# Queries of a hybrid decoder layer in three rounded passes over weight blocks, two token tiles at a time

## The reference, cut to what matters

```python
q = (xt @ w_query).reshape(t, PEER_HEADS, 2, D_HALF)          # 8 heads x 2 halves x 128
scores = einsum('thpd,hpnd->thpn', q, sub_keys)               # 128 keys in each half
sv, si = top_k(scores, 16)
cand_s = sv[:, :, 0, :, None] + sv[:, :, 1, None, :]          # 256 candidates
top_s, pos = top_k(cand_s, 16);  gate = softmax(top_s)        # 8 x 16 experts a token
a = einsum('ted,td->te', expert_u[idx], x)
out = einsum('te,ted->td', gate * gelu(a), expert_v[idx])     # 16384 experts
```

## Time and profile before

| | us |
|---|---|
| median of 3 runs | 1621.68 |
| lowest and highest | 1615.96, 1624.44 |
| the profiled execution | 1623.71 |
| its span, first to last instruction | 1622.0 |
| TensorE busy | 1559.6 (96%) |
| VectorE busy | 1229.5 (76%) |
| ScalarE busy | 703.1 (43%) |
| GpSimd busy | 397.1 (24%) |
| DMA, moved | 425.78 MB, 263 GB/s over the span |

### The profile page before, as it was taken

One profiled execution on the slowest core, in us unless ns is written; L12 is line 12 of the kernel. 1 busy time (PEld: TensorE's weight loads), 2 busy tenths in 40 slices (PEclk: granted clock), 3 DMA queues, 4 the chain that ended last, 5 costly groups with the idle time before them and its releaser, 6 DMA issues.

```text
span 1622.0 us, 23064 instructions
## 1 busy us (share of the span) xinstructions
PE 1559.6 (96%) x7813; PEld 1329.9 (82%) x7813; DVE 1229.5 (76%) x2273; ACT 703.1 (43%) x1289; POOL 397.1 (24%) x326
## 2 busy tenths in 40 slices
PE   6999889999899999999999999899999999999996
PEld 5777755545599998999999999898888888888885
DVE  5789633398469888898789966458888888888888
ACT  4532533213268634885358833233333333333333
POOL 1004200001023300232003344203334444444430
PEclk9999999999999999999999999999999999999998
DMA  8974700001269975799649999959999999999992
GB/s 315 334 238 138 285 1 0 1 1 53 78 234 357 382 248 170 273 364 349 218 143 344 357 388 363 393 194 343 353 335 358 357 354 343 355 358 356 343 328 94
DMA packets 173078, 425.78 MB, mean 263 GB/s; under 512 B 13373, under 2 KB 62525, under 8 KB 169801
## 3 DMA queue, kind: packets, MB, share of 16 engines
q1 hardware_dynamic: 86704, 265.37, 44.2%
q0 software_dynamic: 36864, 134.23, 23.3%
q10 hardware_dynamic: 49432, 25.19, 5.4%
HBM read 372.32 MB, written 52.43 MB: 262 GB/s over the span
## 4 chain that ended last, share of the span: by engine, by line
PE 86%; DVE 6%; DMA 5%; ACT 1%; issue 1%; ACTq 1%; SPq 0%; DVEq 0%
PE bank L1313 10%; PE bank L1314 10%; PE bank L1317 10%; PE bank L1258 10%; PE bank L1259 10%; PE bank L1260 10%; PE bank L1202 7%; PE bank L1273 5%; PE bank L1185 3%; DMA weights<-in_expert_v 2%; DMA weights<-in_w_ada 1%; PE bank L1212 1%; PE bank L1124 1%; PE bank L1120 1%; PE bank L1032 1%
## 5 line engine op out<-in xcount | busy, mean ns | idle before, releaser
L1258 PE MATMUL bank<-h_hi,u_hi 128*128 128x384 f32 x1024 | 350.3, 342 | 11.9 <-ACT ada L883 6.4
L1259 PE MATMUL bank<-h_lo,u_hi 128*128 128x384 f32 x1024 | 345.0, 337 | 0.0
L1260 PE MATMUL bank<-h_hi,u_lo 128*128 128x384 f32 x1024 | 344.7, 337 | 0.0
L1313 PE MATMUL bank<-v_hi,w_hi 128*128 128x512 f32 x768 | 299.4, 390 | 1.1 <-DVE w_lo L1801 1.1
L1314 PE MATMUL bank<-v_lo,w_hi 128*128 128x512 f32 x768 | 298.8, 389 | 0.0
L976 ACT ACTIVATE v_hi<-weights 128x1024 fp32r<-128x1024 f32 x128 | 135.9, 1061 | 330.9 <-PE bank L1317 291.1
L1699 DVE TENSOR_TENSOR u_lo<-weights,u_hi 128x1024 fp32r<-128x1024 f32 x128 | 156.5, 1222 | 120.9 <-PE bank L1260 87.8
L1317 PE MATMUL bank<-v_hi,w_lo 128*128 128x512 f32 x768 | 236.4, 389 | 0.0
L1797 DVE TENSOR_TENSOR v_lo<-weights,v_hi 128x1024 fp32r<-128x1024 f32 x128 | 157.6, 1231 | 94.8 <-ACT v_hi L976 94.8
L1258 PEld LDWEIGHTS bank<-h_hi,u_hi 128*128 128x128 f32 x1024 | 194.7, 190 | 14.0 <-issue 11.2
L1259 PEld LDWEIGHTS bank<-h_lo,u_hi 128*128 128x128 f32 x1024 | 194.9, 190 | 0.0
(11 more groups left out here) (293 smaller groups left out, 2280.2 us busy)
## 6 DMA issues: line engine op xcount, KB each, us to landing
weights<-in_uT SPq DMA_DIRECT2D x128, 512.0 KB
weights<-in_expert_v SPq DMA_DIRECT2D x128, 512.0 KB, 6.9
gates_dense<-weights SPq DMA_DIRECT2D x24, 1024.0 KB
weights<-gates_dense ACTq DMA_DIRECT2D x16, 1536.0 KB
shared<-gelu_dense SPq DMA_DIRECT2D x64, 384.0 KB, 8.1
shared<-in_w_ada SPq DMA_DIRECT2D x16, 1024.0 KB, 5.4
gelu_dense<-weights SPq DMA_DIRECT2D x32, 384.0 KB
gelu_dense<-ada SPq DMA_DIRECT2D x32, 384.0 KB
```

The lines of the kernel that those rows point to most:

```text
L1258: nc.tensor.matmul(a, uh[:, k, :], h2_hi[:, :, k, :], start=(k == 0), stop=False)
L1259: nc.tensor.matmul(a, uh[:, k, :], h2_lo[:, :, k, :], start=False, stop=False)
L1260: ins = nc.tensor.matmul(a, ul[:, k, :], h2_hi[:, :, k, :], start=False, stop=(k == KC - 1))
L1313: nc.tensor.matmul(acc, wh, v_hi[:, r % 2, cols], start=begin, stop=False)
```

## The change

Queries are made transposed at once, so that no query is turned: the weight block of 128 columns is the stationary operand and two token tiles are streamed, 256 columns. They are made in three rounded passes as the products are. The weights come in 16 blocks of 512 KB from an array laid out by block. A ring of eight blocks (raw and lo in one place, hi in another) is filled at the start of attention. Steps 0 to 15 make tiles 0 and 1, in iterations 35 to 50 of the loop; steps 16 to 31 make tiles 2 and 3 behind it, going back through the blocks, so that eight are still there and eight are loaded a second time. Eight blocks are rounded beside heads 5, 8, ..., 26, eight in iterations 38 to 45, and eight in steps 17 to 24. The normed tokens are split on their way out of their transposes' banks. On VectorE tile 0's selection begins with five segments inside the loop; then come five of tile 1, 15 of tile 0, and the other 15 of tile 1 beside the first 17 products. The selection's scratch, the sub-keys, the one-hot rows, the stored products and the gated values lie elsewhere. The dots, the gate loads of ScalarE and the gating of the sparse weights are spread anew.

```diff
-BESIDE = {1: (0,) * 19 + (3,), 2: (1,) * 18 + (0, 0), 3: (1,) * 18 + (0, 0)}
+BESIDE = {1: (0,) * 5 + (1, 1, 1, 2, 1, 1, 1, 1, 1, 1, 2, 1, 1, 1, 1), 2: (1,) * 10 + (0,) + (1,) * 9, 3: (1,) * 10 + (0,) + (1,) * 9}
+FIRST_REST = 3
-LOOP_AT = 12
+LOOP_AT = 14
-DOTS_AT_SEGMENTS = (2, 5, 8, 11, 14)
-DOTS_PER_BODY = {12: 12, 13: 12, 14: 10}
+DOTS_AT_SEGMENTS = {1: (0,) * 9 + (1, 0) * 5 + (1,),
+                    2: (0, 1, 0, 0) * 5, 3: (0, 1, 0, 0) * 5}
+DOTS_AT_LOOP = (2, 2, 2, 1) * 4
+G_LOADS_AT = {(14, 3): 0, (15, 0): 1}
...
+RING_Q = 8
+PER_GROUP = 4
+PAIR_TILES = ((0, 1), (2, 3))
+STEPS_Q = [(0, p) for p in range(HP)] + [(1, p) for p in reversed(range(HP))]
+FIRST_Q = LAST - HP + 1
+ROUNDED_Q = list(range(HP)) + list(reversed(range(RING_Q)))
+ROUND_Q_AT = {5 + 3 * p: p for p in range(RING_Q)}
+ROUND_Q_AT |= {FIRST_Q + 3 + i: RING_Q + i for i in range(RING_Q)}
+EARLY_SEGMENTS = 5
+EARLY_AT = range(LAST - EARLY_SEGMENTS, LAST)
...
-            for g in (2, 3, 0, 1):
-                load_group("w_query", g)
-            sp.wait_ge(a2_done, 1)
+            for p in range(RING_Q):
+                load_wq(p)
+            wait_full(sp, "O", NT - 1)
             sp.dma_start(keysT, sub_keysT).then_inc(keys_in, 16)
+            for p in range(RING_Q):
+                wait_full(sp, "q", 0, p)
+                load_wq(p + RING_Q)
+            for p in range(HP - 1, RING_Q - 1, -1):
+                wait_full(sp, "q", 1, p)
+                load_wq(p - RING_Q)
...
-            wait_full(sp, "qrow", NT - 1, 0)
+            wait_full(sp, "q", 1, 6)
...
-                                wait_full(pool, "turn", 0)
+                                wait_full(pool, "score", NT - 1, 0)
...
+            def round_wq(s):
+                p, uses = ROUNDED_Q[s], s // RING_Q + 1
+                act.wait_ge(wq_in[p % RING_Q], 16 * uses)
+                nc.scalar.activation(wq_hi[p % RING_Q][:, :, :], wq_raw[p % RING_Q].rearrange("p (k n) -> p k n", k=KC),
+                                     ACT.Copy).then_inc(wq_hi_made, 1)
+            def copy_q(step):
+                b = wait_full(act, "q", *STEPS_Q[step])
+                release(nc.scalar.activation(qT[:, step % 2, 0:2 * P], b[:, 0:2 * P], ACT.Copy), "q", *STEPS_Q[step])
...
+                if n in ROUND_Q_AT:
+                    round_wq(ROUND_Q_AT[n])
+                if n >= FIRST_Q:
+                    copy_q(n - FIRST_Q)
+                if n > FIRST_Q:
+                    copy_scored(n - FIRST_Q - 1)
...
+            for step in range(HP, 2 * HP):
+                if 1 <= step - HP <= RING_Q:
+                    round_wq(HP + step - HP - 1)
+                copy_q(step)
+                copy_scored(step - 1)
+                if step == 2 * HP - 3:
+                    wait_full(act, "q", 1, RING_Q // 2)
+                    for r in range(2):
+                        round_u(0, r, True)
...
+            def queries(step):
+                which, p = STEPS_Q[step]
+                tiles = PAIR_TILES[which]
+                pe.wait_ge(wq_lo_made, p + 1 if which == 0 or p >= RING_Q else HP + RING_Q - p)
...
+                for k in range(KC):
+                    at = slice(k * P, (k + 1) * P)
+                    h_hi = h2_hi_first[:, :, at] if which == 0 else h2_hi[:, 1:3, k, :]
+                    nc.tensor.matmul(both_tiles, w_hi_p[:, k, :], h_hi, start=(k == 0), stop=False)
+                    if which:
+                        nc.tensor.matmul(both_tiles, w_hi_p[:, k, :], h2_lo[:, 1:3, k, :], start=False, stop=False)
+                    else:
+                        for t in tiles:
+                            nc.tensor.matmul(both_tiles[:, t, :], w_hi_p[:, k, :], h2_parts(t)[1][:, k, :], start=False, stop=False)
+                    ins = nc.tensor.matmul(both_tiles, w_lo_p[:, k, :], h_hi, start=False, stop=(k == KC - 1))
+                done(ins, "q", which, p)
+            def score(step):
...
+                for half, t in enumerate(PAIR_TILES[which]):
+                    b = start("score", t, g) if j == first else bank[place["score", t, g][0]]
+                    ins = nc.tensor.matmul(b[:, j * P:(j + 1) * P], qT[:, step % 2, half * P:(half + 1) * P], keysT[:, p, :],
+                                           start=True, stop=True)
...
-                if n in FIRST_QUERY:
-                    query(0, QUERY_PAIRS[FIRST_QUERY[n]])
-                if n == SECOND_QUERY:
-                    for pair in QUERY_PAIRS:
-                        query(1, pair)
-            for n in range(2, NT):
-                for pair in QUERY_PAIRS:
-                    query(n, pair)
+                if n >= FIRST_Q:
+                    queries(n - FIRST_Q)
+                if n > FIRST_Q:
+                    score(n - FIRST_Q - 1)
+            for step in range(HP, 2 * HP):
+                queries(step)
+                score(step - 1)
+            score(2 * HP - 1)
...
+            def rest_of_h2(t):
+                hi, lo = h2_parts(t)
+                for s in range(2):
+                    b = wait_full(dve, "h2T", t, s)
...
+            def rest_of_wq(s):
+                b = ROUNDED_Q[s] % RING_Q
+                dve.wait_ge(wq_hi_made, s + 1)
+                tt(wq_lo[b][:, :, :], wq_raw[b].rearrange("p (k n) -> p k n", k=KC), wq_hi[b][:, :, :].bitcast(F32),
+                   ALU.subtract).then_inc(wq_lo_made, 1)
...
-            for _step in first:
-                pass
+            early = [retrieved[1]] * EARLY_SEGMENTS + [retrieved[0]] * (SEGMENTS - EARLY_SEGMENTS)
+            for i, selection in enumerate(early):
+                next(selection, None)
+                if i % 2 and i // 2 < RING_Q:
+                    rest_of_wq(HP + i // 2)
+                if i == SEGMENTS - FIRST_REST:
+                    rest_of_u(0, 0, True)
...
-                for which, rows in ((1, hot_j), (0, hot_i)):
...
+                keys = turned[:, half * HTOK // P % 2, 0:2, at:at + HTOK]
+                tt(hot[:, half % HALVES], iota128.unsqueeze(1).unsqueeze(1).broadcast_to([P, 2, HTOK, P]),
+                   keys.unsqueeze(3).broadcast_to([P, 2, HTOK, P]), ALU.is_equal).then_inc(hot_made, 1)
...
                 if first:
+                    if m == 0:
+                        sparse_weights()
                     loop_add(J, r)
```

More of the change, by code:

```diff
@@ L536, in load_a @@
                     .then_inc(a_in[b], 16)
-            with sp.Fori(LOOP_AT, FEW_DOTS_AT) as I:
-                for r in range(BODY):
-                    loop_product(I, r, True)
             wait_full(sp, "turn", DENSE - 1)
@@ L1275, in build @@
                     ins.then_inc(built, 1)
-            for g in range(4):
-                wait_read(pe, "score", NT - 1, g)
-            pe.wait_ge(h2_lo_made, DENSE)
             m = 0
@@ L1291, in _ @@
                 if d == 0:
-                    for t in range(NT):
-                        for s in range(2):
-                            wait_read(pe, "h2T", t, s)
+                    for g in range(2):
+                        for t in PAIR_TILES[1]:
+                            wait_read(pe, "score", t, g)
                 for h in range(HALVES * d * CHUNKS, HALVES * (d + 1) * CHUNKS):
```

306 lines of the change are left out of this document (144 added, 162 removed).

## The result

The changed kernel takes 1634.39 us, median of five runs (1633.24 to 1635.49); the kernel before, five runs beside it, 1623.02. The ratio is 1.0072, 95% interval 1.0055 to 1.0089: slower, where 1609 was forecast, and 2 us above the top of the range. The profiled execution took 1634.05 us, its span 1632.3 against 1622.0. The 10.3 us between the spans lie as follows; the forecast column is the prediction's own sum cut at the same points.

What follows compares the result with a forecast made beforehand. The prediction took TensorE, busy 96% of the span, as the bound. Its terms, 9.9 + 7 - 1.5 - 1 - 1.7 = 12.7 us, took the profiled 1623.7 to 1611.0, 1609 in the median's terms; 8-in-10 range 1592 to 1632 us.

Steps and rivals of the forecast that it cites:

- Part 2: Attention: rounding eight weight blocks beside the heads delays its end by 8 us, bounds 2 and 18.
- Rival (d): Attention: every rounding is paid in full, 10 us worse than forecast, 1619 us; chance 0.10.
- Part 1: Query steps on TensorE: 120 us with scores against 136, saving 16 us; steps of 3.6 and 2.9 us without scores.
- Rival (c): Query steps: a 256-column pass costs much more than 120 ns, slower from 146 ns, 1678 us at 213 ns; chance 0.08.
- Rival (e): Queries: three passes for four gain little, 104 against 111 us, had the transposes stayed; no chance given.
- Part 3: Attention's end to first products: product 0 at 428 us, product 1 waiting 3.5 us for VectorE; 9.9 us gained.
- Part 4: Products beside the selections: 7 of 8.7 us of holes and slow clock gained, bounds 3 and 11; selection 1 loses 1.5.
- Part 5: Last two bodies: 11 us of loss against 9.8 before, minus 1; sparse weights behind the first output step, minus 1.7.
- the 9.8 us: Last bodies of the kernel before: a 6.4 us TensorE wait plus 3.4 us lost to half clock.
- 30.9 MB at 400 GB/s: Last 16 products: this traffic, some 28 MB needed in time, takes 70 us against 66, a hole of 4 to 6.
- the like stall: Last bodies: ScalarE's second gate load sticks about as long as the kernel before's 13.35 us; sign given as 10 to 20.
- rival (b): Last bodies: DMA engines bound, ScalarE stands 26 us at body 15; 16 us worse than forecast, 1625 us; chance 0.17.

Runs made afterwards that it cites:

- e1_rest_later: Changed kernel with VectorE's rest of each of attention's eight weight blocks one head after ScalarE's rounding: 1618.37 us, 0.9967 to the kernel before.
- e12_rest_behind: The best version: e10_best with VectorE's rest of each of the sixteen first blocks one iteration after ScalarE's rounding, in the tail: 1595.26 us, 0.9846 to the kernel before.
- e5_ve_order: Changed kernel with attention's roundings moved to the tail, plus VectorE's list at the end of the queries reordered: 1612.73 us, 0.9939 to the kernel before.
- e3_before_19: Kernel before with one product, not three, at selection 1's last segment and 19, not 18, beside selections 2 and 3: 1611.18 us, again 1612.98.
- e10_best: Changed kernel, attention's roundings in the tail, VectorE's lists reordered, nine dots beside selections 2 and 3, sparse weights ahead of the first output step: 1601.12 us, 0.9867.
- e9_thin: Changed kernel with attention's roundings in the tail and first-table gathered rows moving an eighth of their bytes: 1604.62 us, 0.9891 to the kernel before.
- e4_gates_apart: Changed kernel with ScalarE's first gate load issued three products earlier: 1636.11 us, 1.0078 to the kernel before.

## Why the prediction was wrong

The granted clock has two levels here, and half clock is the lower one, 1.2 instead of 2.4 GHz.

**The step that failed is Part 2's sum, "Sum 8 us; bounds 2 (all in present idle time) and 18 (eight times 2.3)".** Attention ended 22.6 us later, 0.7 of it from ahead of attention. That is 14.6 of the 23.0 us by which the total is off, and outside the bounds. The mechanism had been named ("ScalarE's queue holds the next exponentials behind it, VectorE's the next row maximum, and TensorE waits for both"), but each rounding was priced as its 2.3 us of work, less a head of cover. Three things were missing. First, the upper bound counted work and not waits: VectorE waits 19 us for ScalarE beside its own work, because the two stand at the same place in both lists. e1_rest_later changes nothing but that order, and 16 us go. Second, an output projection was taken as cover at head 17, and head 23 was counted at 0.5; but there the rest stands ahead of what the projection and the turn wait for, VectorE's copy (L1610) and head norm (L1585), and TensorE waits 3.09 us at 212.26 and 4.73 at 246.54. Third, the sum had no term for the clock: 4.3 us of the delay are TensorE busy at a lower granted clock (0.92 instead of 0.97). This part the better order did not give back, since e1_rest_later's attention is at 0.92 too; what it gave back is idle time. Rival (d), "attention pays every rounding in full", came nearest, at 18 us still 4 short. With the order of e1_rest_later attention ended 6.3 us later than in the kernel before (275.68 against 269.36), so 8 would have been enough for a good order.

**Part 1, the queries: right.** A step of the first pair takes 3.7 us without its scores, forecast 3.6; one of the second pair takes 3.3 us with them, forecast 3.4. Rival (c), a 256-column pass at 146 ns or more, is out, since 24 passes of 256 columns with their own weights start 0.12 us apart. The rule of the Trainium skill, TensorE: Matmul & The Clock Gate, section The mechanism, that a weight load overlaps a running matmul only on another row group, does not agree with these rows. Rival (e) is answered too: with the transposes gone TensorE is busy 151.6 us in the tail against 165.1.

**Part 3, the tail: right in kind, 5.4 us too good.** Product 0 came 156.0 us after attention's end, forecast 150.6. The sum had TensorE busy throughout; it waits 2.93 us for VectorE's copy and 1.40 for a rest of turned tokens (L1705), and runs at half clock from the end of the first wait, 334.2, to 337.1 (1.5 us lost): 5.8 us. Windows of 10 us with this and with the slow clock after product 1's wait:

```profile
330.00:340.00 10.00, 7.07 (x50) 6.91 (x50) 2.42 (x3) 1.33 (x2) 0.00 (x0) 0.83 0.18 52
450.00:460.00 10.00, 5.99 (x26) 5.67 (x26) 9.86 (x36) 4.41 (x6) 4.43 (x5) 0.83 0.36 118
```

The first of the waits is Part 2's mistake once more: Part 3 priced the rests of the tail by VectorE's room, 25 us against 15, and not by what stands behind each. With them in better places the same tail is 151.5 us (e12_rest_behind, 269.5 to 421.0). Product 1's wait on VectorE was forecast at 3.5 us with half clock behind it; it was 4.0, with half clock from its end, 456.4, to 460.0. VectorE's selection was indeed late next; that it was its order is shown by e5_ve_order.

**Part 4, the selections: too careful.** 8.7 us were counted as 7, of which 1.5 came back in selection 1. e3_before_19 shows 9 to 13 us for the edit alone. In the changed kernel three waits of 1.0 us take some of it back; e10_best shows that two of them came with the dots. What is left is some 7 us against the 5.5 of the sum.

**Part 5, the last two bodies: the total right, the step from before not.** 11 us were forecast. Measured are waits of 1.04, 1.66 and 5.63 us and, from 1058.7 to 1064.2, 5.5 us at half clock, 2.8 lost: 11.1.

```profile
1057.00:1065.00 8.00, 6.30 (x22) 6.33 (x23) 4.50 (x7) 2.93 (x4) 4.08 (x4) 0.57 1.04 399
```

But the 9.8 us set against it (6.4 + 3.4) was too much. In the kernel before the clock fell during the wait itself, and TensorE ran at half clock only from 1035.1 to 1038.5, which costs 1.7 and not 3.4 us. So these bodies cost 3 us more than before and not 1, and that is where the product stage, 2.2 us over its forecast, lost most. The selections came out some 1.5 us better and product 1's wait 0.5 us longer than forecast; about 1 us has no place found. The reason given first, 30.9 MB at 400 GB/s, is the one that e9_thin confirms. Of the stuck gate load, given beside it, 4.63 us were left of 13.35, not the like stall of the sum or the 26 us of rival (b), and e4_gates_apart shows that it was a consequence here. The sparse weights were put at 1.7 us and cost 1.8. The 1.74 us at 1160, where VectorE needs the third gate block, had not been foreseen.

## What to carry to other kernels

Work that one engine hands to another, put at the same place in both their lists inside a loop that already passes through both, costs its waits and not its length: put the second half one iteration behind the first, and price it at the place where the loop's own chain goes through. A hole that is due to an order can be tried by that line alone in the kernel before; here one line of the kernel before gave 9 to 13 of the 24 us that the best version gained. And a wait of 3 us in TensorE should be priced with the slower clock behind it, which between e10_best and e12_rest_behind made 4 of the 8.2 us; that is one trace of each.

## What the runs showed of the hardware

- VectorE's rest of a block takes 1.22 us by itself, but 2.04 us at 178.15 in the changed kernel and 1.76 and 1.43 us in e1_rest_later, while GpSimd is at its multiplications (the gating of w_out); the scale next to it takes 2.28 us there, as in the earlier trace rows, where a dot of the same size takes 1.22. GpSimd is the neighbour in time in all of them; that it is the cause was not tried by a run.
- TensorE's rounded passes against the same tokens but other weights start 0.12 us apart at 256 columns; of two 128-column passes that follow each other with the same weights the second starts 0.06 us after the first.
- In the changed kernel the DMA engines were busy without a break from 1000 to 1080 us and moved 401 to 407 GB/s in each 20 us window of it, with a third of the packets (2097 of 6479 from 1020 to 1060 us) being the gate loads'. A full share is not always that rate: 386 GB/s from 1020 to 1040 us in the kernel before, and 363 in e9_thin.
